# Gates of the expert stage once a tile, and dot products that read their rows from SBUF alone

## The reference

```python
def peer_block(h, peer_wq, peer_keys, peer_u, peer_v):
    q = (h @ peer_wq).reshape(n, PEER_HEADS, 2, PEER_HALF)
    s = jnp.einsum('nhpd,hpkd->nhpk', q, peer_keys)
    sc, ix = lax.top_k(s, PEER_TOPK)
    cand = sc[:, :, 0, :, None] + sc[:, :, 1, None, :]      # 16 x 16 sums per head
    cid = ix[:, :, 0, :, None] * N_KEYS + ix[:, :, 1, None, :]
    top, pos = lax.top_k(cand, PEER_TOPK)
    eid = jnp.take_along_axis(cid, pos, axis=-1)
    g = jax.nn.softmax(top, axis=-1)
    act = jax.nn.gelu(jnp.einsum('nhkd,nd->nhk', peer_u[eid], h))
    w = g * act
    return jnp.einsum('nhk,nhkd->nd', w, peer_v[eid])
```

## Time and profile before

| | |
|---|---|
| median of three runs | 4499.94 us (4497.83 to 4509.65) |
| the profiled execution | 4504.35 us, of it the span of the core 4501.9 |
| PE busy | 3405.6 us, 76% |
| DVE busy | 2745.4 us, 61% |
| ACT busy | 954.4 us, 21% |
| GpSimd (POOL) busy | 2437.9 us, 54% |
| software DMA queue (gathers) | 1289.90 MB of 1572.17 |
| mean DMA rate | 349 GB/s |
| mean granted TensorE clock | 0.83 of full speed |

### The profile page before, as it was taken

One profiled execution on the slowest core, in us unless ns is written; L12 is line 12 of the kernel. 1 busy time (PEld: TensorE's weight loads), 2 busy tenths in 40 slices (PEclk: granted clock), 3 DMA queues, 4 the chain that ended last, 5 costly groups with the idle time before them and its releaser, 6 DMA issues.

```text
span 4501.9 us, 46365 instructions
## 1 busy us (share of the span) xinstructions
PE 3405.6 (76%) x16026; PEld 1678.5 (37%) x16026; DVE 2745.4 (61%) x6580; ACT 954.4 (21%) x2013; POOL 2437.9 (54%) x2375
## 2 busy tenths in 40 slices
PE   7998999889889899777989799898844334333455
PEld 4555765455536544343444356443410000000000
DVE  3433420698977776776557875777784487587420
ACT  3453210124423310013444422210100000000000
POOL 0000000146576755556777676565577767777775
PEclk9998999899999899888999999899865555555556
DMA  7775453489899999998999899999999999999998
GB/s 300 263 258 190 184 176 103 163 312 351 299 392 389 411 404 420 392 350 312 383 398 383 315 402 356 408 418 389 390 377 420 419 402 419 420 399 419 419 405 360
DMA packets 422694, 1572.17 MB, mean 349 GB/s; under 512 B 47720, under 2 KB 63464, under 8 KB 411328
## 3 DMA queue, kind: packets, MB, share of 16 engines
q0 software_dynamic: 340384, 1289.90, 72.7%
q1 hardware_dynamic: 78448, 271.38, 16.0%
q10 hardware_dynamic: 3632, 7.94, 0.5%
HBM read 1526.42 MB, written 42.61 MB: 349 GB/s over the span
## 4 chain that ended last, share of the span: by engine, by line
PE 43%; DVE 19%; DMA 15%; POOL 14%; issue 7%; ACT 2%; SPq 0%; DVEq 0%; ACTq 0%; POOLq 0%
DMA peer_v_ring<-in_peer_v,expertsT 7%; PE wide L1878 6%; POOL peer_u_ring L2503 6%; DVE peer_u_ring L2676 6%; PE bank L2570 5%; PE wide L2203 5%; POOL peer_v_ring L2513 5%; DMA peer_u_ring<-in_peer_u,experts 4%; PE wide L1447 4%; PE wide L795 3%; PE wide L1435 3%; POOL w_ring L2513 3%; DMA w_ring<-in_peer_v,expertsT 3%; PE wide L858 2%; PE bank L1878 2%
## 5 line engine op out<-in xcount | busy, mean ns | idle before, releaser
L2503 POOL DMA_INDIRECT peer_u_ring<-in_peer_u,experts x1098 | 1140.7, 1039 | 587.0 <-DVE peer_u_ring L2676 278.1
L2513 POOL DMA_INDIRECT peer_v_ring<-in_peer_v,expertsT x840 | 898.3, 1069 | 459.7 <-PE bank L2570 239.7
L2676 DVE SCALAR_TENSOR_TENSOR peer_u_ring<-peer_u_ring,wide 128x1024 f32<-128x1024 f32 x580 | 698.9, 1217 | 454.4 <-DMA peer_u_ring<-in_peer_u,experts 451.0
L2570 PE MATMUL bank<-peer_v_ring,peer_lone 128*32 128x512 f32 x3360 | 560.2, 745 | 443.5 <-DMA peer_v_ring<-in_peer_v,expertsT 416.5
L2676 DVE SCALAR_TENSOR_TENSOR peer_u_ring<-peer_u_ring,peer_h 128x1024 f32<-128x1024 f32 x518 | 621.1, 1218 | 6.1 <-DMA peer_u_ring<-in_peer_u,experts 4.6
L2570 PE MATMUL bank<-w_ring,peer_lone 128*32 128x512 f32 x1056 | 247.9, 1027 | 343.1 <-DMA w_ring<-in_peer_v,expertsT 340.9
L2570 PEld LDWEIGHTS bank<-peer_v_ring,peer_lone 128*32 128x32 f32 x3360 | 77.6, 117 | 768.8 <-issue 741.0
L2513 POOL DMA_INDIRECT w_ring<-in_peer_v,expertsT x264 | 248.5, 941 | 84.2 <-issue 68.6
L795 PE MATMUL wide<-hT,w_ring 128*128 128x384 f32 x768 | 275.5, 507 | 7.1 <-ACT hT L574 4.0
L2203 PE MATMUL wide<-mT,w_ring 128*128 128x384 f32 x768 | 267.9, 499 | 2.8 <-DMA w_ring<-in_weights 2.8
L1447 PE MATMUL wide<-w_ring,hT 128*128 128x256 f32 x1152 | 261.1, 384 | 0.0
(11 more groups left out here) (330 smaller groups left out, 5108.3 us busy)
## 6 DMA issues: line engine op xcount, KB each, us to landing
w_ring<-in_weights SPq DMA_DIRECT2D x312, 512.0 KB, 6.7
sb_kc<-in_kcT POOLq DMA_DIRECT2D x16, 2048.0 KB, 7.8
sb_vc<-in_vc POOLq DMA_DIRECT2D x16, 2048.0 KB, 8.5
peer_u_ring<-in_peer_u,experts POOLq DMA_INDIRECT x1098, 8.1
mod_w<-in_w_ada SPq DMA_DIRECT2D x15, 1024.0 KB, 11.0
peer_v_ring<-in_peer_v,expertsT POOLq DMA_INDIRECT x840
mod_w_later<-in_w_ada SPq DMA_DIRECT2D x9, 1024.0 KB, 6.7
scores<-sel_sc SPq DMA_DIRECT2D x6, 1024.0 KB, 9.5
```

The costliest lines, as they stand in the source:

```text
L2503: pool.indirect_dma_start(buffer, None, K.A["peer_u"], bass.IndirectOffsetOnAxis(ap=K.ids_of[:, j % CHOSEN, k:k + 1], axis=0)).then_inc(lo ...
L2513: pool.indirect_dma_start(buffer, None, K.A["peer_v"], bass.IndirectOffsetOnAxis(ap=K.ids_of_turned[:, j % CHOSEN, t:t + 1], axis=0)).then ...
L2570: last = pe.matmul(self.F.psum[strip:strip + 32, :], self.lone[:, mark - at:mark - at + 32], self.buffer("v", m)[0][:, c * HALF:(c + 1) * ...
L2676: dve.scalar_tensor_tensor(u, u, 1.0, h2, ALU.mult, ALU.mult, accum_out=self.dots[:, j % 2, k:k + 1]).then_inc(self.dot_done, 1)
```

## The change

It has two parts and one that follows from the second.

The dots read h2 from `peer_h2` in SBUF in every stage. `by_banks`, the copies into the banks and their semaphore go.

The gates are made once a tile. `shifted` gets 128 columns, 16 for each head, and the third piece of `choose` writes its head's. The fourth no longer waits for ACT and makes no gates. `exp_best` takes the exponential of all 128 columns in one instruction, without a sum, when all heads of the tile are chosen; `set_gates` on DVE takes the sums of the heads, their reciprocals, and the product. They stand at slots 70 and 72 of the tile itself, the first tile of a group included. `weigh` waits for the gates by a semaphore.

`act_v` goes: gelu writes `w`, and `weigh` multiplies in place. So gelu waits until PE has turned the `w` of the tile before, and `weigh` no longer does.

```diff
--- before.py
+++ after.py
@@ -40,7 +40,7 @@
 
 SBUF_FROM, SBUF_TO = 16512, 229375
 NU, NV = 8, 6
-BESIDE = (NU + NV + 8) * 4 * D + 4 * (31 + 2 * 16 * 32 + 32 + 1) + 5 * 4 * SLOTS + 3840
+BESIDE = (NU + NV + 8) * 4 * D + 4 * (31 + 2 * 16 * 32 + 32 + 1) + 4 * 4 * SLOTS + 4320
 
 CHUNKS = 3 * SB_PAIRS + 6 * GLA_HEADS + 4 * KC + 8 + 2 * PEER_HEADS
 STICK_AT, GLA_AT, MIX_AT = 0, 3 * SB_PAIRS, 3 * SB_PAIRS + 6 * GLA_HEADS
@@ -572,8 +572,6 @@
             if G.n == 0 and k == 0:
                 act.wait_ge(self.mods.turned, 1)
             act.activation(K.hT[:, k, 0:G.W], out[:, 0:G.W], ACT.Identity, bias=K.modT[:, k, 0:1], scale=K.modT[:, KC + k, 0:1]).then_inc(bank.kept, 1)
-        if G.n:
-            K.select.exp_best(act, GROUPS[G.n - 1].first, PEER_HEADS - 2)
 
 
 C_TURNS = ((0, 1, 2, 3), (4, 5, 6, 7), (8,))
@@ -1134,8 +1132,6 @@
         for n in range(self.pieces(G)):
             if n in keeps:
                 keeps[n](act, G, 0)
-            if n == 3 and G.n:
-                K.select.exp_best(act, GROUPS[G.n - 1].first, PEER_HEADS - 1)
             if not G.sample:
                 tick()
         if G.sample:
@@ -2106,8 +2102,8 @@
 
 
 
-    CHOOSE, READ, SHIFTED, PIECES = 27, 6, 18, 4
-    FROM, EVERY, STEPS_AT, EXP_AT, LOADS_AT = 100, 12, (0, 3, 6, 9), 8, (93, 138)
+    CHOOSE, READ, SHIFTED, PIECES = 25, 6, 18, 4
+    FROM, EVERY, STEPS_AT, EXP_AT, GATES_AT, LOADS_AT = 100, 12, (0, 3, 6, 9), 70, 72, (93, 138)
 
     def __init__(self, K):
         self.K = K
@@ -2130,7 +2126,7 @@
         self.best, self.pos = sb("best", [P, TOPK]), sb("pos", [P, TOPK], U32)
         self.part, self.part_f = sb("part", [P, 2, TOPK], U32), sb("part_f", [P, 2, TOPK])
         self.ids = sb("ids", [P, 2, TOPK])
-        self.shifted, self.e_sum, self.e_inv = sb("shifted", [P, TOPK]), sb("e_sum", [P, 1]), sb("e_inv", [P, 1])
+        self.shifted, self.e_sum, self.e_inv = sb("shifted", [P, SLOTS]), sb("e_sum", [P, PEER_HEADS]), sb("e_inv", [P, PEER_HEADS])
         self.ids_f = sb("ids_f", [P, SLOTS])
         self.cand = self.wide[:, 0:TOPK * TOPK]
         self.cand2 = self.wide[:, TOPK * TOPK:]
@@ -2234,18 +2230,24 @@
                 keep_queries(n)
                 for m in self.keys_behind(n):
                     keep_scores(m)
-            if 0 < h < PEER_HEADS - 1:
-                self.exp_best(act, G.first, h - 1)
         for _ in range(self.PIECES):
             K.tick("ACT", beside)
-        if G.n + 1 == len(GROUPS):
-            for h in range(PEER_HEADS - 2, PEER_HEADS):
-                self.exp_best(act, G.first, h)
-
-    def exp_best(self, act, j, h):
-        n = PEER_HEADS * j + h
-        act.wait_ge(self.chosen, self.CHOOSE * n + self.SHIFTED)
-        act.activation(self.shifted[:, :], self.shifted[:, :], ACT.Exp, accum_out=self.e_sum[:, 0:1]).then_inc(self.exp_done, 1)
+
+    def exp_best(self, act, j):
+        act.wait_ge(self.chosen, self.CHOOSE * PEER_HEADS * (j + 1))
+        act.activation(self.shifted[:, :], self.shifted[:, :], ACT.Exp).then_inc(self.exp_done, 1)
+
+    def set_gates(self, dve, j):
+
+        n = 4 * j
+        by_head = self.shifted[:, :].rearrange("p (h k) -> p h k", h=PEER_HEADS)
+        dve.wait_ge(self.exp_done, n + 1)
+        dve.tensor_reduce(self.e_sum[:, :], by_head, AX_X, ALU.add).then_inc(self.exp_done, 1)
+        dve.wait_ge(self.exp_done, n + 2)
+        dve.reciprocal(self.e_inv[:, :], self.e_sum[:, :]).then_inc(self.exp_done, 1)
+        dve.wait_ge(self.exp_done, n + 3)
+        gates = self.K.gates[:, j % CHOSEN, :].rearrange("p (h k) -> p h k", h=PEER_HEADS)
+        dve.tensor_tensor(gates, by_head, self.e_inv[:, :].unsqueeze(2).broadcast_to([P, PEER_HEADS, TOPK]), ALU.mult).then_inc(self.exp_done, 1)
 
     def choose(self, dve, j, h, s):
 
@@ -2291,7 +2293,7 @@
         did(dve.max(best[:, 8:16], self.cand2))
         so_far()
         did(dve.max_index(pos[:, 8:16], best[:, 8:16], self.cand2))
-        did(dve.tensor_scalar(self.shifted[:, :], best[:, :], best[:, 0:1], None, ALU.subtract))
+        did(dve.tensor_scalar(self.shifted[:, h * TOPK:(h + 1) * TOPK], best[:, :], best[:, 0:1], None, ALU.subtract))
         assert step[0] == self.CHOOSE * n + self.SHIFTED
         yield
         so_far(1)
@@ -2306,14 +2308,11 @@
         did(dve.tensor_tensor(hit, hit, self.at_f[:, :, :].unsqueeze(2).broadcast_to([P, 2, TOPK, TOPK]), ALU.mult))
         so_far()
         did(dve.tensor_reduce(ids[:, :, :].rearrange("p a i -> p (a i)"), hit.rearrange("p a i j -> p (a i) j"), AX_X, ALU.add))
-        dve.wait_ge(self.exp_done, n + 1)
-        did(dve.reciprocal(self.e_inv[:, :], self.e_sum[:, :]))
         so_far()
         cols = slice(h * TOPK, (h + 1) * TOPK)
         did(dve.scalar_tensor_tensor(self.ids_f[:, cols], ids[:, 0, :], float(NKEYS), ids[:, 1, :], ALU.mult, ALU.add))
-        did(dve.tensor_scalar(self.K.gates[:, j % CHOSEN, cols], self.shifted[:, :], self.e_inv[:, 0:1], None, ALU.mult))
         assert step[0] == self.CHOOSE * (n + 1)
-        so_far(1)
+        so_far()
         dve.tensor_copy(self.K.ids_of[:, j % CHOSEN, cols], self.ids_f[:, cols]).then_inc(self.named, 1)
         yield
 
@@ -2373,9 +2372,12 @@
             next(self.pieces)
 
     def exp_beside(self, act, s):
-        j, h, k = self.head_at(s)
-        if h is not None and k == self.EXP_AT:
-            self.exp_best(act, j, h)
+        if s < SLOTS * TILES and s % SLOTS == self.EXP_AT:
+            self.exp_best(act, s // SLOTS)
+
+    def gates_beside(self, dve, s):
+        if s < SLOTS * TILES and s % SLOTS == self.GATES_AT:
+            self.set_gates(dve, s // SLOTS)
 
 
 class Peer:
@@ -2398,12 +2400,11 @@
         self.u_ring, self.v_ring = sb("u_ring", [P, NU, D]), sb("v_ring", [P, NV, D])
         self.h2, self.x1, self.g2, self.ln2, self.prod = sb("h2", [P, 2, D]), sb("x1", [P, D]), sb("g2", [P, D]), sb("ln2", [P, 2 * D]), sb("prod", [P, D])
         self.lone = sb("lone", [P, 31 + 2 * self.REFILL * 32 + 32])
-        self.dots, self.act_v, self.w, self.wT = sb("dots", [P, 2, SLOTS]), sb("act_v", [P, SLOTS]), sb("w", [P, SLOTS]), sb("wT", [P, P])
+        self.dots, self.w, self.wT = sb("dots", [P, 2, SLOTS]), sb("w", [P, SLOTS]), sb("wT", [P, P])
         self.small = sb("stats", [P, 2, 6]), sb("mv", [P, 2]), *(sb(n, [P, 1]) for n in "vyt")
         K.select.place(sb)
         self.u_in, self.v_in = [sem(f"u_in{r}") for r in range(NU)], [sem(f"v_in{r}") for r in range((NV + K.NW) // 2)]
         self.h2_in, self.x1_in, self.g2_in, self.ln2_in, self.y_out = [sem(f"peer_h2_in{n}") for n in range(2)], sem("peer_x1_in"), sem("peer_g2_in"), sem("peer_ln2_in"), sem("peer_y_out")
-        self.copies, self.h2_there = 0, sem("peer_h2_there")
         self.place, self.last_out = self.places(), sem("peer_last_out")
         (self.zeroed, self.dot_done, self.gelu_done, self.w_ready, self.lone_ready, self.v_used, self.summed, self.steps, self.finish_steps, self.ended) = (
             sem("peer_" + n) for n in ("zeroed", "dot_done", "gelu_done", "w_ready", "lone_ready", "v_used", "summed", "steps", "finish_steps", "ended"))
@@ -2440,10 +2441,6 @@
             pool.wait_ge(self.dot_done, had[1] + 1)
         elif had is not None:
             pool.wait_ge(self.v_used, had[1] // 2 + 1)
-
-    def by_banks(self, s):
-
-        return self.K.dots_beside(s) in ("mix", "res", None)
 
     def free_ids(self, dve, j):
         if j >= CHOSEN:
@@ -2595,8 +2592,8 @@
     def gelu(self, act, j):
         act.wait_ge(self.dot_done, SLOTS * (j + 1))
         if j:
-            act.wait_ge(self.w_ready, j)
-        act.activation(self.act_v[:, :], self.dots[:, j % 2, :], ACT.Gelu_apprx_tanh).then_inc(self.gelu_done, 1)
+            act.wait_ge(self.F.full, self.F.full_at["wT", j - 1])
+        act.activation(self.w[:, :], self.dots[:, j % 2, :], ACT.Gelu_apprx_tanh).then_inc(self.gelu_done, 1)
 
     def keep_turned(self, act, j):
         out = self.F.filled(act, ("wT", j))
@@ -2663,15 +2660,6 @@
             if j >= 2:
                 dve.wait_ge(self.gelu_done, j - 1)
         h2 = self.h2[:, j % 2, :]
-        if self.by_banks(n):
-            spare = self.K.wide[2].rearrange("p a n -> p (a n)")
-            if k == 0 or not self.by_banks(n - 1):
-                if n:
-                    dve.wait_ge(self.dot_done, n)
-                self.copies += 1
-                dve.tensor_copy(spare, h2).then_inc(self.h2_there, 1)
-                dve.wait_ge(self.h2_there, self.copies)
-            h2 = spare
         dve.wait_ge(loaded, count)
         dve.scalar_tensor_tensor(u, u, 1.0, h2, ALU.mult, ALU.mult, accum_out=self.dots[:, j % 2, k:k + 1]).then_inc(self.dot_done, 1)
 
@@ -2683,9 +2671,8 @@
 
     def weigh(self, dve, j):
         dve.wait_ge(self.gelu_done, j + 1)
-        if j:
-            dve.wait_ge(self.F.full, self.F.full_at["wT", j - 1])
-        dve.tensor_tensor(self.w[:, :], self.act_v[:, :], self.K.gates[:, j % CHOSEN, :], ALU.mult).then_inc(self.w_ready, 1)
```

(3 more changed lines are left out.)

## The result

The changed kernel takes 4535.36 us (median of 4 runs, 4531.38 to 4546.12) against 4502.03 for the kernel before in the same series: a ratio of 1.0078 with an interval of 1.0058 to 1.0099. The profiled execution took 4546.12 us, the highest of the four, so differences read from its trace are some 10 us larger than those of the medians.

What follows compares the result with a forecast made beforehand. GpSimd's full gather queue was taken to bound the last regime. Terms +105 + 25 - 5 - 12 = +113 us on the profiled 4504.35 us gave 4617, or 4613 in terms of the median; range 4535 to 4700.

Steps and rivals of the forecast that it cites:

- GpSimd's queue bounds the last regime: From 3303 to 4320 us only the expert stage is left; GpSimd's gather requests occupy 990 of 1017 us, slack 27.
- DMA share of 1.02: DMA engines in the last regime, at 414 GB/s: near their end too, but a slower issuer only makes them idle.
- SBUF dots hold gathers: A gather request starting during a dot with two SBUF inputs is held until it ends: 1.98 us instead of 0.94.
- Rival A: No price on GpSimd: last-regime gathers stay at 0.94 us, only DVE's savings remain, about 4475 us; chance 0.09.
- +105 us for the last regime: 398 dots at 0.30 us add 119 us of GpSimd time, less 14 of slack; bounds 53 and 171.
- price of 0.30 us a dot: GpSimd time lost per SBUF dot, from gathers at 1000 to 1310 us: 0.36, less 0.06 for other two-input operations.
- the lower bound I had given: 0.20 us a dot in the last regime: the queue can fall into step with dots and be caught less often.
- 14 assumed: Part of the last regime's added GpSimd time, in us, swallowed by half of its 27 us of slack.
- upper bound of 0.43: Price in us a dot in the last regime, for a queue that stays at the slot length of before.
- +25 for mix and res: Groups 1 and 2: 182 dots at 0.30 us give 55 us, of which half was taken; bounds 0 and 55.
- -12 for the hand-over: Group 1 to group 2: two waits for ACT's exponential, stopping GpSimd 17.50 and 8.81 us, go; bounds 0 and -26.
- -5 for the rest of the gates: First stick stage, DVE busy 262 of 310 us: less DVE work for gates and copies; bounds 0 and -15.

Runs made afterwards that it cites:

- place A: Chips on which the kernel before takes 4502 to 4506 us; the first measurement and the later follow-up runs were there.
- e16: Kernel before with only the gates made once a tile, dots in the banks as before: 4479.69 us against 4505.67, ratio 0.9941.
- e18: The changed kernel run again, unaltered, beside the kernel before: 4535.48 us against 4505.67, ratio 1.0068.
- e13: Kernel before with gates once a tile, dots in banks, value-row gathers moving half rows from tile 5 on: 4468.08 us, ratio to before 0.9920.
- e8: Changed kernel with the last regime's dots replaced by a scaling with one SBUF input: 4649.63 us, ratio to before 0.9947.
- e17: Kernel before with only the dots read from SBUF everywhere, gates once a head: 4555.02 us against 4505.67, ratio 1.0106.
- place B: Chips on which the kernel before takes 4658 to 4674 us; the earlier follow-up runs were there.
- e14: Changed kernel with value-row gathers moving half rows from tile 5 on: 4619.65 us, ratio to before 1.0251.
- e3: Changed kernel with the last regime's dots from the banks again: 4639.09 us against 4657.85 for the kernel before, ratio 0.9960.
- e1: Kernel before with only the gates made once a tile, dots in the banks: 4638.87 us against 4657.85, ratio 0.9966.
- e5: The changed kernel run again, unaltered, beside the kernel before: 4671.35 us against 4674.38, ratio 0.9993.
- e4: Changed kernel with the mix and res dots of groups 1 and 2 from the banks again: 4659.05 us, ratio to before 1.0008.
- e9: Changed kernel with a fill of 512 columns of an unused bank ahead of each last-regime dot: 4810.81 us, ratio to before 1.0319.
- e10: Kernel before with gates once a tile, bank dots, and a 512-column fill ahead of each last-regime dot: 4665.63 us, ratio to before 1.0007.
- e11: Kernel before with only the gates made once a tile, run again: 4636.28 us against 4662.52, ratio 0.9953.
- e12: The changed kernel run once more, unaltered, beside the kernel before: 4659.76 us against 4662.52, ratio 0.9994.

## Why the prediction was wrong, step by step

The measured median, 4535.36 us, lies at the very lower end of the stated range. The mechanism was right; the size of the loss was over three times too large, 113 us for 33.

- **GpSimd's queue bounds the last regime: right in place A**, shown by its 24 to 27 us of slack, by e16 to e18, and by e13, where a quarter less data saves 10 us. So the DMA share of 1.02, which the text left out of the forecast, was rightly left out there. It isn't a property of the kernel alone: in place B the same stretch has 138 us of slack, most of it in stops.
- **SBUF dots hold gathers: right**, e8 and e17 show it, in kind and in place. Rival A falls.
- **+105 us for the last regime: 64 measured. This is the step that failed**, by its price of 0.30 us a dot. It was 0.20 (80 us more busy time over 398 dots: 832 less 751), at the lower bound I had given, for the reason given there: the starts fall into step with the dots, and happen to fall on a dot's end. I had carried a mean from a stage in which PE and ACT jostle the order into a regime with a steadier rhythm. In the mix and res stages the price was indeed 0.30 and 0.25 us a dot (27 us over 90 dots in group 1, 23 over 92 in group 2); in the last regime it depends on where the starts fall, 0.19 to 0.20 with whole rows and 0.43 with half rows in place A. The slack swallowed 80 - 64 = 16 us or so, for 14 assumed. The 64 is from the slowest of the four executions: e18 less e16 gives 56, e17 less before 51. The upper bound of 0.43 was worked out a little low: a start with r us left loses r - 0.14 us where that is above nothing, 0.48 on average and not 0.44, so 0.46 a dot.
- **+25 for mix and res: 9 measured**, and 4 to 6 in the other pairs in place A (e18 less e16, e14 less e13, e17 less before). GpSimd's instructions got as long as forecast (mean 1.12, forecast 1.13), but their own slack hid them; in place B these stages differ by +2 us (e3 less e1) and -7 (e5 less e4), and no price can be told from scatter.
- **-12 for the hand-over: -27 measured**, the whole of the two waits. PE's wait for value rows, which I had named as next in line, shrank with GpSimd's stops: 33.6 us between 1980 and 2060 us before, 15.7 after. Slots 371 to 624 then give some 3 us back. **-5 for the rest of the gates:** right in size by luck. It was forecast for the first stick stage, which gave 1; the 5 us lie ahead of the first dot, which comes at 886 to 893 us in the three kernels with gates once a head and at 884 to 888 in the others, so part of them may be scatter. No run takes them apart.
- Sum: 64 + 9 - 27 - 5 = 41 for the two profiled executions, 42 measured; the medians differ by 33. The three errors point the same way, 41, 16 and 15 us.
- The range began at 4535 with the last regime at +53 but the gains near their middle; taking the low price and the full gain together gives 4500 + 53 - 26 - 5 = 4522, which the range should have reached, since neither had a row against it.

## What to carry to other kernels

Before an operand is moved from PSUM to SBUF, look at what GpSimd does beside it: a dot with two SBUF inputs cost DVE nothing (1221 ns against 1217) and held the gathers that started during it, by up to about 1 us each. If GpSimd's queue is full (busy time plus 0.30 us a request against the stretch), most of that time is the kernel's (56 of 75 us in e18 less e16), else most of it is hidden; count both queues' slack, and don't take one chip's DMA rate for all. Look at a low mean rate in short windows before calling it a slow rate: here it was stops. Where two engines run in a fixed rhythm, a mean cost per event from another stage is a poor estimate: the phase decides. A probe that inserts a step to shift the phase can change more than the phase; count what it catches itself. And take out waits between engines that serve only a value needed much later: one exponential a tile, taken late, was worth 26 us.

## What the runs showed of the hardware that was not expected

- A gather that starts under a dot ends 0.8 us after the dot, so it seems to be held near its beginning; one that starts with 0.1 us of the dot left loses nothing, with 0.2 us left less than 0.1. A second dot right behind the first doesn't hold it further: of the 784 gathers of the changed kernel's last regime 3 took 2.0 us or more. But some operations right ahead of a dot do lengthen the hold: the fill of e9, and in the changed kernel a fill of 1.76 us at 1300.15 us, under which a gather that starts at 1300.87 takes 2.92 us. Why stays open.
- The mean rate at which gathers land differs by place: 413 GB/s in the last regime of e16 and 373 in e1, the same instructions. That stretch is 109 us longer there (1122 against 1013), more than anything in this change. It is made of some 20 stops; between them both run at about 420 GB/s. What makes the stops stays open.
- A fill of 512 columns of an unused bank, 0.48 us, cost 29 us with bank dots (e10 against e11) and 151 us with SBUF dots (e9 against e12), where it moved gathers into dots and caught others itself.
